# A decoder layer with routed experts on one core: first stage reordered, expert routing by marked values, table products in pairs, an expert load moved in its queue

## The reference

```python
def route(x2, w_router, router_bias):
    t = x2.shape[0]
    scores = jax.nn.sigmoid((x2 @ w_router).astype(jnp.float32))
    biased = scores + router_bias.astype(jnp.float32)
    grp = biased.reshape(t, N_GROUPS, N_EXPERTS // N_GROUPS)
    grp_score = jnp.sum(lax.top_k(grp, 2)[0], axis=-1)
    _, gidx = lax.top_k(grp_score, TOPK_GROUPS)
    gmask = jnp.sum(jax.nn.one_hot(gidx, N_GROUPS), axis=1) > 0
    emask = jnp.repeat(gmask, N_EXPERTS // N_GROUPS, axis=1)
    _, eidx = lax.top_k(jnp.where(emask, biased, -jnp.inf), TOP_K)
    gw = jnp.take_along_axis(scores, eidx, axis=-1)
    gw = gw / jnp.sum(gw, axis=-1, keepdims=True) * ROUTED_SCALE
    return eidx, gw
...
    z = h @ lw['w_in']
...
    ffn = (swiglu(x2, lw['w_s_gate'], lw['w_s_up'], lw['w_s_down'])
           + routed_experts(x2, eidx, gw, lw['w_e_gate'], lw['w_e_up'], lw['w_e_down']))
    ple = jax.nn.sigmoid(h @ lw['w_ple_gate']) * (p @ lw['w_ple_proj'])
```

## Time and profile before

| | us |
|---|---|
| median of 3 runs | 1259.24 (1258.89 to 1259.71) |
| profiled execution, its own time | 1259.58 |
| its span, first to last instruction | 1257.7 |
| TensorE busy | 1217.8 (97% of the span) |
| VectorE busy | 511.7 (41%) |
| ScalarE busy | 316.5 (25%) |
| GpSimd busy | 159.5 (13%) |
| mean granted clock of TensorE | 0.995 of full speed |

### The profile page before, as it was taken

How to read it: one execution, slowest core, us unless ns; L and a number is a source line. 1 busy time by engine, 2 the same in 40 slices (tenths; PEclk the granted TensorE clock), 3 DMA queues, 4 the chain that set the end, 5 groups by cost and what they waited for, 6 DMA issues and landing times.

```text
span 1257.7 us, 23359 instructions
## 1 busy us (share of the span) xinstructions
PE 1217.8 (97%) x8776; PEld 978.3 (78%) x8777; DVE 511.7 (41%) x1123; ACT 316.5 (25%) x576; POOL 159.5 (13%) x226
## 2 busy tenths in 40 slices
PE   7999999999999999999899999999999999999987
PEld 7999978999999999998899665556555566666643
DVE  4666773432444323566885112211222221111137
ACT  4364653322212222316012111111111111111121
POOL 0200000000000000004235212111121121212200
PEclk9999999999999999999999999999999999999999
DMA  9212223223232232615428999999999999999986
GB/s 264 83 58 68 68 51 68 68 67 101 68 95 75 72 114 67 212 26 205 180 89 328 420 418 420 420 420 420 420 421 419 420 421 418 419 422 421 421 343 285
DMA packets 98656, 307.31 MB, mean 244 GB/s; under 512 B 11244, under 2 KB 62404, under 8 KB 72840
## 3 DMA queue, kind: packets, MB, share of 16 engines
q1 hardware_dynamic: 85332, 275.20, 56.6%
q0 software_dynamic: 12304, 28.60, 5.9%
q10 hardware_dynamic: 948, 2.50, 0.6%
HBM read 294.45 MB, written 26.94 MB: 256 GB/s over the span
## 4 chain that ended last, share of the span: by engine, by line
PE 59%; DMA 33%; DVE 5%; issue 1%; DVEq 1%; ACT 0%; SPq 0%; POOL 0%; ACTq 0%; POOLq 0%
PE proj L1065 32%; DMA w_exp<-in_w_e_down_dram 31%; PE att L1468 5%; PE proj L1257 4%; PE proj L1487 3%; PE proj L1398 3%; PE att L1179 1%; PE att L1141 1%; DMA fold<-expert_rows 1%; PE att L1266 1%; PE proj L1352 1%; PE proj L1408 1%; PE att L1192 1%; PE proj L1382 1%; PE proj L1091 1%
## 5 line engine op out<-in xcount | busy, mean ns | idle before, releaser
L1468 PE MATMUL att<-w_exp,xt 128*64 128x256 f32 x2560 | 286.4, 380 | 2.4 <-DMA w_exp<-in_w_e_up_dram 2.3
L1468 PEld LDWEIGHTS att<-w_exp,xt 128*64 128x64 f32 x2560 | 207.6, 137 | 89.9 <-issue 27.2
L1065 PE MATMUL proj<-h_hi,w_hi 128*128 128x288 f32 x768 | 168.0, 300 | 0.3 <-DVE w_lo L470 0.3
L1065 PE MATMUL proj<-h_lo,w_hi 128*128 128x288 f32 x768 | 164.1, 295 | 0.0
L1065 PE MATMUL proj<-h_hi,w_lo 128*128 128x288 f32 x768 | 164.1, 295 | 0.0
L1487 PE MATMUL proj<-w_exp,ht_e 128*64 128x512 f32 x640 | 146.2, 597 | 9.7 <-issue 5.7
L1065 PEld LDWEIGHTS proj<-h_hi,w_hi 128*128 128x128 f32 x768 | 122.3, 189 | 6.1 <-issue 4.6
L1065 PEld LDWEIGHTS proj<-h_lo,w_hi 128*128 128x128 f32 x768 | 123.6, 189 | 0.0
L1065 PEld LDWEIGHTS proj<-h_hi,w_lo 128*128 128x128 f32 x768 | 123.6, 189 | 0.0
L470 DVE TENSOR_TENSOR w_lo<-w_raw,w_hi 128x2048 fp32r<-128x2048 f32 x33 | 75.6, 2292 | 92.4 <-ACT w_hi L460 87.2
L1487 PEld LDWEIGHTS proj<-w_exp,ht_e 128*64 128x64 f32 x640 | 50.4, 136 | 77.9 <-issue 75.3
(11 more groups left out here) (386 smaller groups left out, 1859.2 us busy)
## 6 DMA issues: line engine op xcount, KB each, us to landing
w_exp<-in_w_e_gate_dram SPq DMA_DIRECT2D x64, 1024.0 KB
w_exp<-in_w_e_up_dram SPq DMA_DIRECT2D x64, 1024.0 KB
w_exp<-in_w_e_down_dram SPq DMA_DIRECT2D x64, 1024.0 KB
w_raw<-in_w_in_dram SPq DMA_DIRECT2D x21, 1024.0 KB
part<-expert_rows SPq DMA_DIRECT2D x8, 1536.0 KB, 21.4
w_raw<-in_w_in_dram SPq DMA_DIRECT2D x8, 512.0 KB
w_raw<-in_w_attn_out_dram SPq DMA_DIRECT2D x8, 512.0 KB
w_raw<-in_w_conv_out_dram SPq DMA_DIRECT2D x4, 1024.0 KB
```

Of the source, the lines that this page charges most:

```text
L1065: last = nc.tensor.matmul(proj[:, 2 * i + a, 0:HALF], lhs, x[:, c, a * HALF:(a + 1) * HALF], start=(c == 0 and n == 0), stop=(c == KC - 1 ...
L1468: last = nc.tensor.matmul(att[e * SLOT:(e + 1) * SLOT, m, 0:FF], xt[:, c, e * SLOT:(e + 1) * SLOT], weights[e][:, c, :], start=(c == 0), s ...
```

## The change

**First stage.** The identity is loaded ahead of tile 0. TensorE starts with 13 matmuls of a zeroed tile `warm` (GpSimd clears it), whose results are not used. After six quads come 7 more of them, then a quarter of the first products (high by high, first half of the tokens), then the four last quads, then the rest. VectorE makes both `h_hi` and `h_lo` of quads 4 and 5, and ScalarE splits the first weights after its fourth quad.

**Routing.** `match_replace` marks the best groups and the best experts with a value in place, and `sel` comes from a comparison with that value; `max_index` and the one-hot matrix `hot` come after `sel`. The rank matrix lies in its own PSUM bank (`att` 2), so TensorE no longer waits for `hs_ready` before it. The running sum over pairs is one scan. The weights of all five tiles are worked out at once, ahead of the first table. TensorE takes the tables two by two, with one gate unit behind each two; before, there was a unit behind each.

**Loads.** SP waits for `routed` and loads three parts of pair 1 ahead of the wait for units 5 to 9 and `load_gate(3)`; part 4 no longer waits for `hs_hd`.

```diff
+            pe.wait_ge(x_zero, 1)
+            for _ in range(N_WARM):
+                nc.tensor.matmul(att[:, 3, 0:P], warm[:, :], warm[:, :], start=True, stop=True)
...
             pe.wait_ge(ld_x, 16)
...
+            token_quads(0, 6)
+            for _ in range(N_BRIDGE):
+                nc.tensor.matmul(proj[:, 3, 0:P], warm[:, :], warm[:, :], start=True, stop=True)
             pe.wait_ge(hi_done, 1)
+            pe.wait_ge(x_hi, 6)
+            for i in range(2):
+                first_products(0, 0, i)
+            token_quads(6, len(QUADS))
```

```diff
+            sp.wait_ge(routed, 1)
+            load_parts(1, 1, range(3))
             sp.wait_ge(u_ready, 2 * NT)
             load_gate(3)
-            sp.wait_ge(routed, 1)
-            load_parts(1, 1, range(3))
             sp.wait_ge(ppo_added, 1)
-            load_parts(1, 1, range(3, 4))
+            load_parts(1, 1, range(3, 5))
             sp.wait_ge(hs_hd, 1)
-            load_parts(1, 1, range(4, 6))
+            load_parts(1, 1, range(5, 6))
```

```diff
+            nc.vector.memset(gbest[:, :, TOPG:8], 4 * BIG)
+            dve.drain()
             for t in range(NT):
-                nc.vector.max_index(gidx[:, t, :], gbest[:, t, :], gsum[:, t, :])
-            dve.drain()
-
-            nc.vector.tensor_copy(gidx_f[:, :, :], gidx[:, :, 0:TOPG])
-            dve.drain()
-            for t in range(NT):
-                nc.vector.tensor_tensor(ghot[:, t, :, :], iota64[:, 0:NGRP].unsqueeze(1).to_broadcast([P, TOPG, NGRP]),
-                                        gidx_f[:, t, :].unsqueeze(2).to_broadcast([P, TOPG, NGRP]), ALU.is_equal)
-            dve.drain()
-            nc.vector.reduce_sum(gmask[:, :, :], ghot[:, :, :, :].rearrange("p t i g -> p t g i"), AX.X)
-            dve.drain()
-            nc.vector.tensor_scalar(gmask[:, :, :], gmask[:, :, :], BIG, -BIG, ALU.mult, ALU.add)
+                nc.vector.match_replace(gmask[:, t, :], gbest[:, t, :], gsum[:, t, :], BIG)
+            dve.drain()
+            nc.vector.tensor_scalar(gmask[:, :, :], gmask[:, :, :], BIG, -BIG, ALU.not_equal, ALU.mult)
...
+            nc.vector.memset(ebest[:, :, TOPK:8], 4 * BIG)
+            dve.drain()
+            for t in range(NT):
+                nc.vector.match_replace(replaced[:, t, :], ebest[:, t, :], biased[:, t, :], BIG)
+            dve.drain()
+            nc.vector.memset(replaced[NS:P, NT - 1, :], 0.0)
+            dve.drain()
+            nc.vector.tensor_scalar(sel[:, :, :], replaced[:, :, :], BIG, None, ALU.is_equal).then_inc(sel_ready, 1)
...
-            cur = npass_f
-            for s in range(5):
...
+            nc.vector.tensor_tensor_scan(cums[:, :], npass_f[:, :], no_steps[:, :], 0.0, ALU.add, ALU.add)
...
+            pick(wj[:, :], scores)
...
             for m in range(NTK // TPAIR):
-                if m == 2:
+                if m == 4:
                     shared_act(1)
-                if m % 2 == 0:
-                    weights_of(m // 2)
```

```diff
+            pe.wait_ge(hs_ready, 1)
             for u in range(N_AHEAD):
                 gate_unit(u)
-            pe.wait_ge(rank_read, 1)
             for m in range(NTK // TPAIR):
                 table_products(m)
-                gate_unit(N_AHEAD + m)
-            for u in range(N_AHEAD + NTK // TPAIR, 3 * NT):
+                if m % 2 == 1:
+                    gate_unit(N_AHEAD + m // 2)
+            for u in range(N_AHEAD + NTK // TPAIR // 2, 3 * NT):
                 gate_unit(u)
```

More of the change, by code:

```diff
@@ L56 @@
 N_AHEAD = 3
+N_WARM = 13
+N_BRIDGE = 7
+ON_DVE = (4, 5)
 RING = (0, 1, 2)
@@ L331, in decoder_step @@
         npass_f = rsm("npass_f", [P, NPE], F32)
-        cums = [rsm(f"cums{i}", [P, NPE], F32) for i in range(2)]
+        cums = rsm("cums", [P, NPE], F32)
         slot_j, col_j, code_j = (rsm(n, [P, NTK], F32) for n in ("slot_j", "col_j", "code_j"))
@@ L678, in _ @@
         def _(pool):
+            nc.gpsimd.memset(warm[:, :], 0.0).then_inc(x_zero, 1)
             pool.wait_ge(kv_tok_ready, 1)
@@ L721, in _ @@
             pool.wait_ge(x2_out, 16 * NT)
[L722 removed]
+            pool.wait_ge(x_zero, 2)
             def gather(k, i, n):
@@ L1087, in first_products @@
-            def first_products(i, n, a, c):
-                w, x = ((w_hi, h_hi), (w_hi, h_lo), (w_lo, h_hi))[n]
-                lhs = w[:, 0, :].rearrange("p (c n) -> p c n", c=KC)[:, c, i * P:(i + 1) * P]
-                return nc.tensor.matmul(proj[:, 2 * i + a, 0:HALF], lhs, x[:, c, a * HALF:(a + 1) * HALF],
-                                        start=(c == 0 and n == 0), stop=(c == KC - 1 and n == 2))
-            pe.wait_ge(hi_done, 1)
-            for a in range(2):
-                pe.wait_ge(x_hi, (6, len(QUADS))[a])
-                for i in range(2):
-                    for c in range(KC):
-                        first_products(i, 0, a, c)
+            pe.wait_ge(x_zero, 1)
@@ new lines, in _, with token_quads @@
+            for _ in range(N_WARM):
+                nc.tensor.matmul(att[:, 3, 0:P], warm[:, :], warm[:, :], start=True, stop=True)
+            def token_quads(first, last_n):
+                for n in range(first, last_n):
+                    t, c = QUADS[n]
+                    pe.wait_ge(tile_in[t], 16)
+                    if n >= 4:
+                        pe.wait_ge(x_lo, n - 3)
+                    w = ntok(t)
+                    for j in range(4):
+                        k = 4 * c + j
+                        last = nc.tensor.transpose(att[:, n % 4, j * P:j * P + w], x_tok[0:w, t, k * P:(k + 1) * P],
+                                                   ident[0:w, 0:w])
+                    last.then_inc(tr_x, 1)
@@ new lines, in first_products @@
+            def first_products(n, a, i):
+                w, x = ((w_hi, h_hi), (w_hi, h_lo), (w_lo, h_hi))[n]
+                for c in range(KC):
+                    lhs = w[:, 0, :].rearrange("p (c n) -> p c n", c=KC)[:, c, i * P:(i + 1) * P]
+                    last = nc.tensor.matmul(proj[:, 2 * i + a, 0:HALF], lhs, x[:, c, a * HALF:(a + 1) * HALF],
+                                            start=(c == 0 and n == 0), stop=(c == KC - 1 and n == 2))
+                return last
+            pe.wait_ge(ld_x, 16)
@@ new lines, in _ @@
+            token_quads(0, 6)
+            for _ in range(N_BRIDGE):
+                nc.tensor.matmul(proj[:, 3, 0:P], warm[:, :], warm[:, :], start=True, stop=True)
+            pe.wait_ge(hi_done, 1)
+            pe.wait_ge(x_hi, 6)
+            for i in range(2):
+                first_products(0, 0, i)
+            token_quads(6, len(QUADS))
+            pe.wait_ge(x_lo, 6)
+            for i in range(2):
+                first_products(1, 0, i)
+            pe.wait_ge(x_hi, len(QUADS))
+            for i in range(2):
+                first_products(0, 1, i)
@@ L1100, in _ @@
             pe.wait_ge(x_lo, len(QUADS))
+            for i in range(2):
+                first_products(1, 1, i)
             pe.wait_ge(w_ready, 1)
             for i in range(2):
-                for n in range(1, 3):
-                    for c in range(KC):
-                        for a in range(2):
-                            last = first_products(i, n, a, c)
+                for a in range(2):
+                    last = first_products(2, a, i)
                 last.then_inc(mm_ready[i], 1)
@@ L1362, in _ @@
             pe.wait_ge(sc_ready, 1)
[L1363 to L1364 removed]
+            shared_half(1, 0, range(2))
             pe.wait_ge(sel_ready, 1)
[L1367 removed]
             for t in range(NT):
[L1369 to L1373 removed]
+                for k in range(t + 1):
+                    nc.tensor.matmul(rank_out(t), (ones_b if k < t else tri_b)[:, :], sel[:, k, :],
+                                     start=(k == 0), stop=(k == t))
+            for k in range(NT):
+                last = nc.tensor.matmul(rank_out(NT), ones_b[:, :], sel[:, k, :], start=(k == 0), stop=(k == NT - 1))
             last.then_inc(rank_ready, 1)
[L1375 removed]
+            shared_half(1, 0, range(2, KC))
+            pe.wait_ge(rank_read, 1)
+            shared_half(1, 1, range(KC)).then_inc(su_ready, 1)
             def table_products(m):
@@ L1868, in _ @@
             nc.vector.memset(scores[NS:P, NT - 1, :], 0.0)
+            nc.vector.memset(no_steps[:, :], 0.0)
             dve.wait_ge(sc_ready, 1)
```

103 lines of the change are left out of this document (33 added, 70 removed).

## The result

| | before | after |
|---|---|---|
| median, us | 1259.09 (20 runs, 1256.92 to 1260.87) | 1261.67 (20 runs, 1259.46 to 1264.7) |
| ratio | | 1.0022 (95%: 1.0016 to 1.0028) |
| profiled execution, its own time / span | 1259.58 / 1257.7 | 1261.61 / 1259.8 |

The change makes the kernel 2.6 us slower by the medians, 2.0 by the two profiled executions. The forecast was 1258.8. The loss is 0.22%, small, but its interval excludes none.

What follows compares the result with a forecast made beforehand. TensorE, busy 97% of the span, was taken as the bound. Terms -0.75 + 1.3 + 0.2 - 1.2 = -0.45 took the profiled execution to 1259.1, 1258.8 us as a median; 8-in-10 range 1254.3 to 1261.6.

Steps and rivals of the forecast that it cites:

- Step 3: Tables in pairs: GpSimd's split holds table 9, TensorE waits 2.7 to 3.6 us; +1.3 us.
- Step 2: Routing up to the first table: table 0 begun 1.4 us earlier, TensorE idle 3.3 against 3.41, no clock fall.
- rival 2: TensorE's clock falls in the new waits before the first tables and table 9: +3.6 us, 1262.4; chance 0.11 at both.
- block 3: Gate block 3's load, issued some 3 us later, reaches TensorE within 0.5 us either way: +0.2 us.
- idle at the tables: TensorE's waits at the routing tables: 3.3 us at the first two plus 3.2 at table 9, against 3.41 before.
- clock and tables behind a wait: At the first table and next gate unit: the 1.8 us lost before to the low clock would go.
- Step 1: First stage: first product at 13.0 instead of 14.70, end at 27.3 against 28.05; -0.75 us.
- rival 3: First stage: warm start and new products do nothing, quads bound by their tiles; +0.75, 1259.6; within the middle's 0.53.
- Step 4: Loads: three parts of pair 1 flow while DMA engines idle; +0.2 for block 3, -1.2 for the lead.
- the lead: Expert stage: earlier loads put pair 2 1.2 us ahead (bounds 0.5 and 3), cutting TensorE's weight waits: -1.2 us.
- Both signs named: Expert loads: TensorE's down-weight waits under 2.5 us in total, and DMA engines idle right before pair 2's loads.

Runs made afterwards that it cites:

- the later split: Changed kernel with GpSimd splitting gate block 2 one unit later: 1260.36 us; with the loads also as before: 1256.31 us.
- single tables: Changed kernel with tables one by one, a gate unit behind each: 1269.88 us; with the loads also as before: 1254.90, then 1256.47 us.
- the fourth gate unit in the wait: Kernel with single tables and loads as before, given four gate units ahead of table 0 in place of three: 1256.89 us.

## Why the prediction was wrong, by its steps

**Step 3 held and was half of the matter.** The wait for table 9 was forecast at 2.7 to 3.6 us and is 3.28, by the mechanism named: four instructions, each held by a piece of GpSimd's split. That it is the split is shown by moving it alone, with the loads as before: 6.4 us, and the same four instructions at a third of their time.

**The step that failed is the clock.** Step 2 says "I take no fall" for the first wait, and the sum has none for table 9. In the trace both came, at 0.7 and 2.9 us, together the 3.6 us that rival 2 puts on them; it got 0.11. That its 1262.4 is within 0.8 of the result is in part luck, since other terms were off both ways, as the table below shows. The row by which the fall was ruled out cannot show one: 3.3 us at 0.50 in a stretch of 400 us leave a mean of 0.996, printed as 1.00. The wait of 1.7 in the earlier trace rows is the one at 174 us, and the stretch of 2 us behind it shows 0.50. The sum also took the 1.8 us of the kernel before as clock alone; 0.26 of them are the table behind a wait (1.18 in place of 0.92), whatever the clock.

How often a wait is followed by a fall, in all 18 traces: waits of 1.62 to 1.66 us at 174 us, 7 of 18; waits of 2.7 us at table 0, 8 of 12; waits of 3.3 to 3.8 us at table 0 or table 9, 5 of 5. Where the wait was filled with matmuls or with a gate unit there is none, 4 of 4 (one at table 9, three at table 0). That idleness brings the fall is well supported by this; what decides in a given execution stays open. That a fall costs its own length in the whole is not shown: filling either wait with matmuls gave nothing measurable, as block 3 or the experts' weights were the next bound. The 6.4 us of the later split are wait and fall together.

Term by term, trace of after less trace of before:

| | forecast, us | trace, us |
|---|---|---|
| first stage (at 174 us) | -0.75 | -0.1 |
| fall at 176 us that stayed away | none | -1.6 |
| TensorE done with gate unit 2 (0.82 of it the wait for `sel`) | 0 | +1.0 |
| idle at the tables: 2.73 + 1.20 + 3.28 against 3.41 | +3.1 | +3.8 |
| clock and tables behind a wait: 0.70 + 2.94 against 1.83 | -1.8 | +1.8 |
| block 3 | +0.2 | 0 |
| expert stage | -1.2 | -2.9 |
| sum | -0.45 | +2.0 |

**Step 1 gave nothing in the stage.** The first product was forecast at 13.0 and began at 13.65. The three instructions of VectorE took 0.68 us each, about the 0.65 estimated, but began at 11.50 and not at 11.0. The end, forecast at 27.3, is 28.16. That is rival 3: the quads are bound by their tiles. What the forecast calls a cold clock shows in the times of the transposes alone; the granted clock of that stretch is 1.00 in both kernels. Yet putting the old stage back cost 2.6 to 3.9 us in three kernels with the new routing and 0.3 with the old. The traces give 0.1 to 0.3 us to the stage itself and the rest to falls and waits far behind it, which the same kernel shows in one trace and not in the next. The fall at 176 us, in 3 of 5 traces with the old stage and 4 of 13 with the new, would be worth some 0.5 us on average at 1.6 us each, an estimate from few traces. What ties the rest to the stage stays open.

**Step 2 was right in its length and wrong in what it brings.** `sel` was forecast by 601.2 and ended at 601.3, table 0 begun at 622.7 and is at 622.25, TensorE at 624.8 to 625.4 and is at 624.77. But all three stand in a trace that is 1.66 us early. Without that, TensorE gets table 0 at 626.43, later than before. What was left out: the last instruction ahead of `sel_ready` met GpSimd's split of block 1 (1.39 us for one of 320 elements, 0.60 in the one trace in which it got through sooner), and TensorE, which had done its 12 products, waited 0.82 us for it. The routing alone measures +0.2 and -0.3 us in two tries. The second wait, for table 1, was forecast at 0.9 and came.

**Step 4 had its signs right and its cause only in part.** The forecast was -1.2 for the lead; by pass 11 the kernel after has 2.1 back. Both signs named came: the waits for down weights are 2.4 us up to 1200 us, under the 2.5 named (3.1 in the whole), and the DMA engines are at 0.05 from 685.0 to 685.6 us, right before pair 2's load. But with the loads as before and the pairs kept the lead is nearly as good (41.6 us), since the pairs bring `routed` forward: the median moved by 1.1, within the uncertainty. The cost, "+0.2" for block 3, held only because TensorE was late anyway. As soon as table 9 was in time it became 4.0 us (1260.36 against 1256.31), and with single tables 15 (1269.88 against 1254.90).

So the 2.6 us come out of the medians as: first stage and routing together -2.9 (1256.2, the kernel with single tables and old loads), pairs with the early split +6.5 (1262.74), loads -1.1.

## What to carry to other kernels

When a reordering makes two products wait on end for one engine, look at what GpSimd does beside it at that time; moving one line of GpSimd's program was worth 6.4 us. A wait of TensorE of 2.7 us or more is to be priced with a fall of the clock behind it, which took 0.7 to 2.7 us in these traces, as the likely case and not as a rival; and such a fall is looked for in stretches of a few us. And a stage that is sped up ahead of a stream of loads pays only as far as the stream is ahead. With single tables the fourth gate unit in the wait gave nothing, and TensorE waited for weights instead; with the tables in pairs, which ask for pair 1 earlier, the split moved and the fourth unit in the wait, the kernel is 5.3 us faster than before.

## What was not expected of the hardware

- One kernel's executions differ in where the clock falls: behind the same wait of 2.73 us the next 30 matmul records of one kernel (the new routing alone) took 4.04 us in one trace and 5.60 in the other, and behind 1.65 us of idleness ahead of 176 us the fall cost 1.6 us or nothing. The runs of one kernel spread over some 3 to 6 us, as much as the effects looked for or more.
- The same code gets through GpSimd's split quickly or slowly: `sel` took 0.60 us in one trace and 1.39 in that of the kernel after, and the first table came 2.1 us earlier.
- A cast of 31 numbers on one partition took 1.27 us beside GpSimd's pieces, 0.16 without.
- MATCH_REPLACE8 on 64 elements takes 0.21 us, as FIND_INDEX8 does; a scan of 32 takes 0.22.
